# Attention pipeline, norms inside the projections, and one mixer stage in a two-block network on one Trainium2 core

## The chip, the core and the metric

The kernel runs on one core of one Trainium2 chip. A core has five engines that run beside each other and meet only at semaphores: TensorE (PE in the profile, PEld for its weight loads) multiplies matrices into PSUM, VectorE (DVE), ScalarE (ACT) and GpSimd (POOL) work on vectors, and SyncE (SP) issues nearly all transfers. The metric is the device time of one execution in microseconds (us). Everything is in 32-bit floating point.

## What is computed

Two blocks over 256 latent tokens of width 1024 follow each other; the first also carries 256 context tokens. Cut to what matters here (`rms` is a norm over the features with a gain):

```
first:  u = rms(h) * (1 + scale) + shift          # layer 0, 512 tokens
        h += gate * (delta_rule(u) gated) @ w_out
        u = rms(h) * (1 + scale) + shift          # layer 1
        q, k, v, z = split(u @ w_in);  q, k = rms per head;  rope on the latent ones
        h += gate * (softmax(q k / sqrt(128)) v * silu(z)) @ w_out      # 8 query, 2 key heads
        x = rms(h)                                # final norm of the first block
second: p = rms(x) @ w_in                         # SSD, RWKV, HGRN and 3 x 1024 gate columns
        y_b = branch_b(p_b) @ w_branch_b          # b = SSD (normed), RWKV, HGRN
        x += (sum_b sigmoid(p_gate_b) * y_b) @ w_out
        g, v = split(rms(x) @ ffn_w_in);  x += (silu(g) * v) @ ffn_w_down
        return rms(x)
```

## The kernel before

Features lie on the 128 partitions, tokens along the free axis, so a tensor of width 1024 is eight tiles `[128, tokens]`. `h` and `u` hold 512 columns (context, latent). All weights come as one stream of 512 KB chunks, in the order in which they are used, into a ring of two sets of six slots (`Stream`). Each chunk is eight 128x128 blocks, one output tile of a 1024-deep product. SyncE loads the next group while TensorE uses the present one; how far it is ahead is set by waits on a count of finished tiles.

The program is a row of stages (`stage`): in each, every engine has its own list of instructions in a fixed order, written out by hand, with semaphore waits between the lists; at a stage's end all engines meet. Nothing plans the order at run time. On VectorE and ScalarE each instruction in a `Chain` waits for the one before it.

Around the change:

- `linear` is a projection stage: TensorE accumulates output tiles in PSUM banks, VectorE takes each away with the given `evacuate`. `project`, `residual_linear` (adds to `h`) and `gated_linear` (multiplies a gate) are made of it.
- `feature_norm` is a stage of its own: eight squares on ScalarE, seven adds on VectorE, column sums by TensorE, mean on VectorE, power -1/2 on GpSimd (`inverse_root`, L148), `spread` by TensorE, eight or sixteen scalings on VectorE (L455), for the modulated norm also sixteen biases on ScalarE (L430). It runs six times behind the prelude: after the DeltaNet output, after the attention output (final norm of the first block), before the SSD projection, on the SSD output ahead of the RWKV inputs, ahead of the FFN, and at the end.
- Attention: all 16 query and z tiles and 4 key and value tiles are projected first; `attention_keys` is a stage; `attention_heads` is a loop of four stages, one for each pair of query heads, each from the query norm to the gated output.
- `rwkv_inputs` makes the RWKV operands out of 14 projected tiles, with small products on TensorE.
- `BesideGroups` and `Beside` put products of a later projection into TensorE's list between the steps of a stage; ScalarE copies the tiles out, or takes tanh(x/2) of them for a gate. The 24 gate tiles are made beside `hgrn_heads`. The SSD heads make 16 tiles for RWKV beside themselves, of which two are products with columns of zeros.
- The end of the second block's mixing: three `gated_linear` stages, one stage on VectorE that adds the three, `residual_linear`, the norm, `swiglu`, `residual_linear`, the norm, and `finish`, which stores `out` with one DMA.

Of the kernel before, what the change touches and what calls it, by code (L numbers as in the profile page):

```python
# [16 lines left out]
F32 = mybir.dt.float32  # L17
# [4 lines left out]
P = 128  # L22
D = 1024
# [176 lines left out]
class Stream:  # L200
# [89 lines left out]
    def in_stage(self, count, per_group, summed, block):  # L290


        first = self.set

        @block.sync
        def _(sp):
            for g in range(count):
                other = (first + g + 1) % 2
                if g:
                    sp.wait_ge(summed, g * per_group)  # L300
# [4 lines left out]
            sp.wait_ge(summed, count * per_group)  # L305
# [105 lines left out]
def feature_norm(nc, bank, C, h, u, g_cols, mod, streams, sq, rs, gs):  # L411


    lo, n = streams[0][0], sum(x[1] for x in streams)
    tiles = n // P
    with stage(nc, "squared added summed mean root spread scaled") as (s, block):
        @block.gpsimd
        def _(pool):
            inverse_root(nc, pool, C, rs[:, 0:tiles], s["mean"], s["root"])

        @block.scalar
        def _(act):
            for k in range(KT):
                nc.scalar.activation(sq[:, k, 0:n], h[:, k, lo:lo + n], ACT.Square).then_inc(s["squared"], 1)  # L424
            if mod is not None:
                link = Chain(act, s["act_own"])
                for k in range(KT):
                    for i, (t0, tn, m) in enumerate(streams):
                        act.wait_ge(s["scaled"], len(streams) * k + i + 1)
                        link(nc.scalar.activation(u[:, k, t0:t0 + tn], u[:, k, t0:t0 + tn], ACT.Identity, bias=mod[:, k, m:m + 1]))  # L430

        @block.tensor
        def _(pe):
            pe.wait_ge(s["added"], KT - 1)
            column_sums(nc, C, bank[0], sq[:, 0, :], tiles).then_inc(s["summed"], 1)
            pe.wait_ge(s["root"], 1)
            spread(nc, C, bank[1], rs, tiles).then_inc(s["spread"], 1)

        @block.vector
        def _(dve):  # L440
            link = Chain(dve, s["dve_own"])
            if mod is not None:
                for _, _, m in streams:
                    link(nc.vector.tensor_scalar(gs[:, :, m], mod[:, 8:16, m], 1.0, None, ALU.add))
                    link(nc.vector.tensor_tensor(gs[:, :, m], gs[:, :, m], g_cols, ALU.mult))
# [2582 lines left out]
```

## Time and profile before

| | |
|---|---|
| median of 3 runs | 2381.48 us (2377.84 to 2381.9) |
| the profiled execution | 2380.35 us |
| its span in the profile | 2378.6 us |
| TensorE busy, weight loads busy | 2021.5, 1484.7 us |
| VectorE, ScalarE, GpSimd busy | 1059.6, 577.9, 76.0 us |
| mean granted TensorE clock | 0.914 of full speed |
| moved by DMA | 183.72 MB |

The span runs from the first to the last record of the profiled execution. Busy time is time in which an engine has an instruction at work, not waiting. The granted clock is the share of TensorE's full 2.4 GHz; it has two levels, 1.0 and 0.5. A 32-bit product is two records in the profile. In a timeline, a line may merge several instructions of one kind (x8), and the brackets give the idle time ahead of it and what ended it.

### The profile page before, as it was taken

The numbers are of one execution on the slowest core, as the hardware profiler recorded it, in microseconds if no ns is written. First come the engines' busy times: TensorE is split into PE (matmuls) and PEld (weight loads), VectorE is DVE, ScalarE is ACT, GpSimd is POOL, SyncE is SP. The second block draws the span as 40 slices with busy tenths as digits, with TensorE's granted clock in tenths as the row PEclk, the third lists the DMA queues.
The fourth block names the chain that finished last, engine by engine and source line by source line (L and its number), as shares of the span: only waits on it lengthen the run. The fifth ranks groups of instructions, "written<-read, shape, count | busy, mean of one in ns | idle before, by whom it ended". The sixth has DMA issues, their size and how long they took to land. (4 is left out here: it accounts for less than half of the span.)

```text
span 2378.6 us, 40862 instructions
## 1 busy us (share of the span) xinstructions
PE 2021.5 (85%) x16732; PEld 1484.7 (62%) x16732; DVE 1059.6 (45%) x2136; ACT 577.9 (24%) x1248; POOL 76.0 (3%) x51
## 2 busy tenths in 40 slices
PE   5889898998989898896955687867989999879997
PEld 2356666565666656345633576644776798768886
DVE  4345756656575665102134318776445433211101
ACT  2033443434344343002012103222332321000000
POOL 0000110101010010000000000000000000000000
PEclk9889998999999998897967888986999999989998
DMA  8610101011010100212300132111012222324443
GB/s 332 266 54 2 55 1 56 1 55 55 2 55 1 55 1 2 106 71 76 107 0 0 71 118 107 71 66 41 29 55 94 82 101 85 110 106 156 162 159 124
DMA packets 50339, 183.72 MB, mean 77 GB/s; under 512 B 5744, under 2 KB 7152, under 8 KB 49648
## 3 DMA queue, kind: packets, MB, share of 16 engines
q1 hardware_dynamic: 50160, 181.18, 20.6%
q8 instruction: 132, 2.16, 0.4%
q14 instruction: 47, 0.39, 0.1%
HBM read 180.11 MB, written 1.05 MB: 76 GB/s over the span
## 5 line engine op out<-in xcount | busy, mean ns | idle before, releaser
L826 PE MATMUL banks<-u,w_ring 128*128 128x512 f32 x768 | 357.0, 602 | 6.6 <-PEq L195 6.6
L406 PE MATMUL banks<-u,w_ring 128*128 128x256 f32 x1088 | 248.4, 390 | 13.5 <-PEq L195 13.5
L406 PEld LDWEIGHTS banks<-u,w_ring 128*128 128x128 f32 x1088 | 212.4, 197 | 47.2 <-issue 17.8
L826 PEld LDWEIGHTS banks<-u,w_ring 128*128 128x128 f32 x768 | 141.7, 193 | 137.6 <-issue 134.5
L485 PE MATMUL banks<-u,w_ring 128*128 128x256 f32 (+1 forms) x640 | 158.7, 412 | 17.2 <-PEq L195 17.2
L485 PEld LDWEIGHTS banks<-u,w_ring 128*128 128x128 f32 x640 | 125.7, 197 | 49.9 <-issue 33.6
L485 PE MATMUL banks<-gated,w_ring 128*128 128x512 f32 (+1 forms) x384 | 141.0, 530 | 3.0 <-PEq L195 3.0
L485 PEld LDWEIGHTS banks<-gated,w_ring 128*128 128x128 f32 x384 | 74.0, 193 | 69.6 <-issue 66.3
L424 ACT ACTIVATE sq<-h 128x256 f32<-128x256 f32 (+1 forms) x40 | 14.5, 444 | 349.7 <-PEq L195 349.7
L853 DVE SCALAR_TENSOR_TENSOR acc<-raw,hc,acc 128x512 f32<-128x512 f32 x128 | 96.2, 752 | 4.6
L382 PE MATMUL banks<-u,w_ring 128*128 128x256 f32 x384 | 88.2, 380 | 0.0
L485 PE MATMUL banks<-ffn,w_ring 128*128 128x256 f32 x352 | 77.9, 385 | 3.0 <-PEq L195 3.0
L485 PEld LDWEIGHTS banks<-ffn,w_ring 128*128 128x128 f32 x352 | 68.1, 194 | 12.8 <-issue 3.4
L382 PEld LDWEIGHTS banks<-u,w_ring 128*128 128x128 f32 x384 | 70.6, 191 | 8.2
L1046 PE MATMUL banks<-const_base,a_t 128*128 128x128 f32 x128 | 28.8, 420 | 54.9 <-PEq L195 29.8
L1202 ACT ACTIVATE acc<-banks 128x512 f32<-128x512 f32 x80 | 47.8, 597 | 94.9 <-PE banks L1070 94.9
L2893 DVE SCALAR_TENSOR_TENSOR h<-banks,mod,h 128x256 f32<-128x256 f32 x24 | 10.9, 481 | 133.0 <-PE banks L485 133.0
L2855 DVE SCALAR_TENSOR_TENSOR ffn_tanh<-ffn_tanh,banks 128x256 f32<-128x256 f32 x22 | 9.2, 418 | 136.7 <-ACT ffn_tanh L2847 136.7
L1275 DVE TENSOR_TENSOR acc<-acc,banks 128x512 f32<-128x512 f32 x80 | 55.0, 688 | 26.7 <-PE banks L1086 24.8
L1271 DVE TENSOR_TENSOR y<-banks,const_base 128x512 f32<-128x512 f32 x80 | 55.3, 691 | 25.3 <-PE banks L1061 24.0
L1225 ACT ACTIVATE dec<-banks,hs 128x128 f32<-128x128 f32 x128 | 47.0, 367 | 70.7 <-PE banks L1143 67.6
L1086 PE MATMUL banks<-y,acc 64*64 64x64 f32 x2560 | 57.6, 225 | 7.6 <-ACT acc L1202 6.1
(468 smaller groups left out, 3248.8 us busy)
## 6 DMA issues: line engine op xcount, KB each, us to landing
w_ring<-in_w SPq DMA_DIRECT2D x323, 512.0 KB, 6.0
h<-in_h SPq DMA_DIRECT2D x2, 2048.0 KB, 9.5
const_base<-in_const SPq DMA_DIRECT2D x1, 1216.0 KB, 5.4
const_part<-in_const SPq DMA_DIRECT2D x1, 1024.0 KB, 4.9
out<-u SPq DMA_DIRECT2D x1, 1024.0 KB, 4.8
const_part<-in_const SPq DMA_DIRECT2D x1, 640.0 KB, 4.4
const_part<-in_const SPq DMA_DIRECT2D x1, 512.0 KB, 3.5
w_rows<-in_rows SPq DMA_DIRECT2D x1, 512.0 KB, 5.7
```

What stands on the lines that cost most here:

```text
L382: mm = self.nc.tensor.matmul(place, self.st.chunk(g % 2, slot)[:, P * k:P * k + P], self.src(k), start=(k == 0), stop=(k == KT - 1))
L406: last = nc.tensor.matmul(out, lhs[k], rhs[k], start=(k == 0), stop=(k == n - 1))
L424: nc.scalar.activation(sq[:, k, 0:n], h[:, k, lo:lo + n], ACT.Square).then_inc(s["squared"], 1)
L485: mm = nc.tensor.matmul(bank[q % banks][:, 0:n_tok], st.chunk(h, c)[:, P * b:P * b + P], src(k), start=(k == 0), stop=(k == k_tiles - 1))
L826: mm = nc.tensor.matmul(self.places[m % len(self.places)][:, :], st.slot(m)[:, P * k:P * k + P], u[:, k, :], start=(k == 0), stop=(k == KT ...
L853: link(nc.vector.scalar_tensor_tensor(out, raw[:, m, :, i:i + SEQ], hc[:, 5 * m + i:5 * m + i + 1], out, ALU.mult, ALU.add), self.s["conv" ...
L1046: mm = nc.tensor.transpose(tile(bank[2 * (c % 2) + c // 2], t), tile(a_t[:, c, :], t), C("ident"))
L1086: mm = nc.tensor.matmul(block_of(bank[2 * d + j], t, hb), invt_c[half(j), d, 2 * t + hb, :], prod[half(j), d, hb, t, :], start=True, stop= ...
L1202: link(nc.scalar.activation(invt_c[:, d].rearrange("p s e -> p (s e)"), bank[4 + d][:, :], ACT.Copy), s["t_out"])
L1225: link(nc.scalar.activation(tile(vn[:, d, :], j), tile(bank[2], 2 * d + j), ACT.Copy, scale=col(BETA, 2 * j + d, t)), s["vn_ready"] if j a ...
L1271: link(nc.vector.tensor_tensor(prod[:, d], both(sums(2 * d, 256)), mask(d, lv), ALU.mult), s["p_ready"])
L1275: link(nc.vector.tensor_tensor(by_chain(inv[:, d]), by_chain(inv[:, d]), both(sums(2 * d, 256)), ALU.subtract), s["t_ready"])
```

## The change

Five things are done together. The norms lose their stage: `residual_norm` is a projection whose squares and adds follow each tile, with root and scaling at its end (`NormTail`); for the end of the first block `DoubleTail` gathers the sums for both norms that follow each other in one pass. Attention is one stage: keys, four pairs in a software pipeline, and the eight z tiles in TensorE's list between its first steps; the key and value tiles are projected first. `rwkv_inputs` takes the norm of the SSD output and six gate tiles (two more come from the SSD heads in place of the zeros), so `hgrn_heads` makes 16 gate tiles. These first eight gates lie in `h`, whose content goes to a DRAM tensor `hold` meanwhile and comes back in the mixer. The three branches, their sum and the output projection are one stage (`mixer_out`). The output is stored in eight pieces behind the last scaling.

```diff
+class NormTail:
+    def square(self, act, link, k):
+        act.wait_ge(self.s["evacuated"], self.base + k + 1)
+        if k >= 3:
+            act.wait_ge(self.s["added"], k - 2)
+        out = self.sq[:, k % 2, 0:self.n] if k else self.acc[:, 0:self.n]
+        link(self.nc.scalar.activation(out, self.tile(k), ACT.Square), self.s["squared"])
...
+    def sums(self, pe):
+        pe.wait_ge(self.s["added"], KT - 1)
+        column_sums(self.nc, self.C, self.bank, self.acc, self.tiles).then_inc(self.s["sums"], 1)
+        pe.wait_ge(self.s["root"], 1)
+        spread(self.nc, self.C, self.bank, self.rs, self.tiles).then_inc(self.s["spread"], 1)
...
+class DoubleTail(NormTail):
...
+    def mean(self, dve, link):
...
+        dve.wait_ge(self.s["root"], 1)
+        link(self.nc.vector.tensor_tensor(self.rs2[:, :], first, first, ALU.mult))
...
+def residual_norm(nc, st, bank, C, count, per_body, src, k_tiles, h, lo, n, gate, work, finish, loaded=None, make=NormTail):
...
+            for m in range(KT):
+                dve.wait_ge(s["used"], m + 1)
+                gate(m, bank[m % banks], link, s["evacuated"])
+                if m:
+                    tail.add(dve, link, m - 1)
+            tail.add(dve, link, KT - 1)
+            tail.mean(dve, link)
+            more["vector"](dve, link)
...
 # modulated norm, after the DeltaNet output
+                            for k in range(KT):
+                                link(nc.vector.tensor_tensor(u[:, k, :], h[:, k, :], bank[7][:, :], ALU.mult), s["scaled"])
...
+                                    link(nc.scalar.activation(u[:, k, t0:t0 + tn], u[:, k, t0:t0 + tn], ACT.Identity,
+                                                              bias=nxt[:, k, c:c + 1], scale=gs[:, k, c:c + 1]))
...
 # attention, TensorE's list
+                extra.products(pe, 4)
+                pe.wait_ge(s["k_sq"], ATT_KV)
+                column_sums(nc, C, bank[7], ksq, ATT_KV * TT)
...
+                extra.products(pe, 12)
+                pe.wait_ge(s["root"], 1)
+                for h in range(ATT_KV + 1):
+                    spread(nc, C, bank[h], rc[:, TT * h:TT * h + TT], TT).then_inc(s["spread"], 1)
+                extra.products(pe, 6)
...
+                query_turn(0)
+                query_sums(1)
+                extra.products(pe, 18)
+                query_roots(1)
+                for n in range(4):
+                    scores(0, n)
+                extra.products(pe, 8)
+                query_turn(1)
+                extra.products(pe, 16)
+                for i in range(pairs):
                     for n in range(4):
+                        turn(i, n)
+                        if i + 1 < pairs:
+                            scores(i + 1, n)
+                        if i and n == 0:
+                            outs(i - 1, 1)
+                        if i + 2 < pairs and n == 0:
+                            query_sums(i + 2)
+                        if i + 2 < pairs and n == 1:
+                            query_roots(i + 2)
+                        if i + 2 < pairs and n == 3:
+                            query_turn(i + 2)
+                    outs(i, 0)
+                outs(pairs - 1, 1)
...
 # rwkv_inputs, TensorE's list
+            extra.products(pe, 2 * KT)
+            pe.wait_ge(*loaded)
...
+            pe.wait_ge(s["x_out"], 1)
+            extra.products(pe, KT)
...
+            pe.wait_ge(s["n_added"], KT - 1)
+            column_sums(nc, C, bank[6], sq[:, 0, :], ST).then_inc(s["n_summed"], 1)
+            extra.products(pe, KT)
+            pe.wait_ge(s["a_in"], 4)
+            extra.products(pe, KT)
             pe.wait_ge(s["root"], 1)
...
+            pe.wait_ge(s["n_root"], 1)
+            spread(nc, C, bank[6], roots, ST).then_inc(s["n_spread"], 1)
...
 # build
+        start_loads(nc, [(hold, early)], late)
...
-                hgrn_heads(nc, st, bank, banks, C2, cs, p_hg, lf, kf, cc("hgrn_norm_w"), yh, work, latent, gates, 24, 6)
+                hgrn_heads(nc, st, bank, banks, C2, cs, p_hg, lf, kf, cc("hgrn_norm_w"), yh, work, latent, gates[:, 8:24, :], 16, 4)
...
+def mixer_out(nc, st, bank, C, branches, early, gates, h, hold, reloaded, work, u, g_cols):
+    units = [(b, m) for b in range(4) for m in range(KT)]
+    through = [0, 4, 8, 16, 24, 28, 32]
...
+            for q, (b, m) in enumerate(units):
+                if q >= banks:
+                    pe.wait_ge(s["evacuated"], q + 1 - banks)
...
+                    if b == 3 and m == 0:
+                        pe.wait_ge(s["mixed"], k + 1)
...
+                if b == 3 and m == 0:
+                    dve.wait_ge(reloaded, 16)
+                dve.wait_ge(s["used"], q + 1)
+                if b < 3:
+                    link(nc.vector.scalar_tensor_tensor(own, own if b else early[:, m, :], 1.0, ps, ALU.add, ALU.mult), s["evacuated"])
+                    if b:
+                        link(nc.vector.tensor_tensor(mixed, mixed, own, ALU.add), s["mixed"] if b == 2 else None)
...
 # last norm and store
+                        for k in range(KT):
+                            sp.wait_ge(s["scaled"], k + 1)
+                            sp.dma_start(out[:, SEQ * k:SEQ * k + SEQ], u[:, k, CTX:TOK]).then_inc(late, 16)
```

## Rows read from the trace of the kernel before

**Rows 1.** the page, part 1: busy us, share of the span, instructions

```profile
PE 2021.5 (85%) x16732; PEld 1484.7 (62%) x16732; DVE 1059.6 (45%) x2136; ACT 577.9 (24%) x1248; POOL 76.0 (3%) x51
```

**Rows 2.** windows: busy us (instructions) by engine, granted clock, DMA share, GB/s

```profile
1205.00:1314.00 109.00, 65.95 (x216) 38.82 (x216) 47.07 (x108) 27.04 (x56) 4.03 (x4) 0.74 0.00 0
1600.00:1641.00 41.00, 21.82 (x84) 12.94 (x84) 30.42 (x52) 13.77 (x24) 4.46 (x2) 0.58 0.00 1
1880.00:2000.00 120.00, 120.00 (x782) 111.90 (x781) 48.34 (x147) 26.55 (x55) 2.27 (x3) 1.00 0.21 80
2015.00:2113.00 98.00, 88.27 (x384) 75.88 (x384) 18.89 (x34) 0.00 (x0) 0.00 (x0) 0.93 0.36 129
```

**Rows 3.** timeline, first output projection to the next: start, us, engine, work

```profile
1081.96 0.88 DVE L2893 SCALAR_TENSOR_TENSOR h<-banks,mod,h 128x256 f32<-128x256 f32 x2 [12.86 <-PE banks L485]
1083.39 4.26 ACT L424 ACTIVATE sq<-h 128x512 f32<-128x512 f32 x8 [123.37 <-PEq L195]
...
1089.75 1.87 PE L155 MATMUL banks<-const_base,sq 128*128 128x1 f32 x8 [7.83 <-DVE sq L448]
...
1094.25 8.23 DVE L455 SCALAR_TENSOR_TENSOR u<-h,gs,banks 128x256 f32<-128x256 f32 x16 [2.37 <-PE banks L162]
1094.77 8.65 ACT L430 ACTIVATE u<-u,mod 128x256 f32<-128x256 f32 x16 [7.11 <-DVE u L455]
1103.93 57.51 PE L485 MATMUL banks<-u,w_ring 128*128 128x256 f32 x256 [9.79 <-PEq L195]
...
1109.68 0.42 DVE L2879 COPY pqz<-banks 128x256 f32<-128x256 f32 x1 [7.20 <-PE banks L485]
1113.13 0.42 DVE L2879 COPY pqz<-banks 128x256 f32<-128x256 f32 x1 [3.03 <-PE banks L485]
```

**Rows 4.** timeline, last key/value tile to the attention's output projection

```profile
1190.23 0.69 DVE L2879 COPY pkv<-banks 128x512 f32<-128x512 f32 x1 [6.18 <-PE banks L485]
...
1191.86 1.06 PE L1358 MATMUL banks<-const_base,pkv 128*128 128x128 f32 x8 [1.67 <-PEq L2583]
...
1193.18 3.45 PE L155 MATMUL banks<-const_base,sq 128*128 128x1 f32 x16 [0.26 <-ACT sq L1349]
...
1314.92 27.89 PE L485 MATMUL banks<-gated,w_ring 128*128 128x256 f32 x128 [1.50 <-PEq L195]
```

**Rows 5.** timeline, attention output, two norms, SSD projection

```profile
1342.85 0.48 DVE L2893 SCALAR_TENSOR_TENSOR h<-banks,mod,h 128x256 f32<-128x256 f32 x1 [2.97 <-PE banks L485]
...
1344.64 3.19 DVE L448 TENSOR_TENSOR sq<-sq 128x256 f32<-128x256 f32 x7 [1.30 <-ACT sq L424]
...
1350.79 4.10 DVE L455 SCALAR_TENSOR_TENSOR h<-h,cols,banks 128x256 f32<-128x256 f32 x8 [1.63 <-PE banks L162]
...
1366.99 43.58 PE L485 MATMUL banks<-u,w_ring 128*128 128x256 f32 x192 [4.77 <-PEq L195]
```

**Rows 6.** timeline, SSD end to RWKV heads; last, GpSimd in RWKV output

```profile
1586.96 0.42 DVE L1765 TENSOR_TENSOR u<-ssd_th,ssd_z 128x256 f32 x1 [0.16 <-DVE ssd_th L1763]
...
1630.29 3.93 POOL L148 TENSOR_TENSOR rc_rw<-rc_rw,const_base 128x16 f32<-128x16 f32 x1 [36.18 <-DVE rc_rw L1875]
...
1640.43 0.52 POOL L1914 MEMSET rw_m_t<- 128x512 f32 x1 [6.20 <-POOLq L195]
...
1829.53 2.89 POOL L148 TENSOR_TENSOR st_rw<-st_rw,const_base 128x16 f32<-128x16 f32 x1 [188.58 <-DVE st_rw L2314]
```

**Rows 7.** timeline, mixer branches, output projection, FFN

```profile
2015.21 29.92 PE L485 MATMUL banks<-u,w_ring 128*128 128x256 f32 x128 [1.64 <-PEq L195]
...
2082.76 30.28 PE L485 MATMUL banks<-gates,w_ring 128*128 128x256 f32 x128 [7.47 <-PEq L195]
...
2125.32 54.95 PE L406 MATMUL banks<-u,w_ring 128*128 128x256 f32 x246 [4.78 <-PEq L195]
```

**Rows 8.** the DMA view: issues, KB each, median us to landing

```profile
out<-u SPq DMA_DIRECT2D x1, 1024.0 KB, 4.8
...
rope<-in_rope SPq DMA_DIRECT2D x1, 256.0 KB, 2.8
```

More of the change, by code:

```diff
@@ L288, in groups, with in_stage @@
             decorate(run)
-    def in_stage(self, count, per_group, summed, block):
+    def in_stage(self, count, per_group, summed, block, through=None, between={}):
         first = self.set
+        through = through or [per_group * g for g in range(count + 1)]
         @block.sync
@@ L299, in _ @@
                 if g:
[L300 removed]
+                    sp.wait_ge(summed, through[g])
                 if g == count - 1:
@@ L407, in accumulate @@
     return last
[L411 to L445, printed above, removed]
-            for k in range(1, KT):
-                dve.wait_ge(s["squared"], k + 1)
-                link(nc.vector.tensor_tensor(sq[:, 0, 0:n], sq[:, 0, 0:n], sq[:, k, 0:n], ALU.add), s["added"])
-            dve.wait_ge(s["summed"], 1)
-            link(nc.vector.tensor_scalar(rs[:, 0:tiles], bank[0][:, 0:tiles], 1.0 / D, EPS, ALU.mult, ALU.add), s["mean"])
-            dve.wait_ge(s["spread"], 1)
-            for k in range(KT):
-                for t0, tn, m in streams:
-                    scale = gs[:, k, m:m + 1] if mod is not None else g_cols[:, k:k + 1]
-                    link(nc.vector.scalar_tensor_tensor(u[:, k, t0:t0 + tn], h[:, k, t0:t0 + tn], scale,
-                                                        bank[1][:, t0 - lo:t0 - lo + tn], ALU.mult, ALU.mult), s["scaled"])
@@ L1478, in attention_heads @@
-        with nc.Fori(0, ATT_Q // 4) as pair:
-            for half in range(2):
-                body(pair * 2 + half, pair)
+        q_of = lambda i: flat(pqz[:, 2 * i:2 * i + 2, :])
+        z_of = lambda i: flat(pqz[:, ATT_Q + 2 * i:ATT_Q + 2 * i + 2, :])
+        tile = lambda a, t: a[:, P * t:P * t + P]
+        angle = lambda n: rope[:, SEQ * n:SEQ * n + SEQ]
+        over = lambda a: a.unsqueeze(1).to_broadcast([P, 2, SEQ])
+        roots_of = lambda i: rq[:, i % 2, :] if i else rc[:, ATT_KV * TT:]
@@ L1819, in _ @@
                     mm.then_inc(s["spread"], 1)
+            pe.wait_ge(s["n_root"], 1)
+            spread(nc, C, bank[6], roots, ST).then_inc(s["n_spread"], 1)
+            pe.wait_ge(s["gd"], 1)
+            for t in range(ST):
+                pe.wait_ge(s["x_out"], 4 + t)
+                nc.tensor.matmul(bank[(7, 4)[t]][:, :], ps[:, 13, P * t:P * t + P], g_up[:, :], start=True,
+                                 stop=True).then_inc(s["g_raw"], 1)
+            extra.products(pe, KT)
             pe.wait_ge(s["rk_ready"], 1)
@@ L2705, in build @@
         C, _ = tiles_of((), None)
[L2707 to L2713 removed]
+        hold = nc.dram_tensor("hold", (P, KT, SEQ), F32).ap()
+        early = h[:, :, CTX:TOK]
+        start_loads(nc, [(hold, early)], late)
         p_rw = p_hg = sb("p_next", [P, 16, SEQ])
```

627 lines of the change are left out of this document (422 added, 205 removed).

## The prediction

> **What bounds the kernel now.** I read the page's busy shares first: TensorE 85%, VectorE 45%, ScalarE 24% [rows 1]. That says only that TensorE is the engine to follow. The windows by stage come next, because the average hides two kinds of stage. In the HGRN stage TensorE is busy all the time at full clock (120.00 of 120 us, clock 1.00); in the attention bodies it is busy 65.95 of 109 us at clock 0.74, in the RWKV input stage 21.82 of 41 us at 0.58 [rows 2]. The reader should see that TensorE sets the end in the first kind, and a chain through all engines in the second. The chain view covers only the last norm and says nothing of the rest. So the timelines around each place that the diff touches come last, and give the terms. All matrix work is in order on TensorE, so time is saved wherever TensorE has nothing to do while a norm or a softmax runs.
>
> The unit of the sum: one 128x256 output tile of eight products takes 3.45 us (two evacuations at 1109.68 and 1113.13). The first after an idle stretch took 5.75 us (from 1103.93 to 1109.68) [rows 3], so leaving idle costs 2.3 us.
>
> **A. DeltaNet output and modulated norm.** Before, the last product ends at 1081.95 and TensorE's next projection starts at 1103.93, 22.0 us later [rows 3]. After, seven of eight squares and six of seven adds lie beside later tiles. Behind the last product remain: the gated add 0.88, one 512-wide square 0.6, one add 0.7 (seven of them fill most of the 6.4 from 1083.39 to 1089.75), handovers 0.2, which puts the column sums at 1084.4 where they stood at 1089.75. The path on to the scaling (mean, power, spread) is kept. The 16 ScalarE activations (8.65 us for 16) still come last, since eight 512-wide multiplies on VectorE take 5.8. First scaling op 0.7 where it was 0.5. Gain 5.3 - 0.2 = 5.1 us. Bounds 3 to 6.
>
> **B. Attention.** Before, from the last key/value evacuation's end (1190.92) to the output projection (1314.92) 124.0 us pass, and the eight z tiles, which are now done inside the attention, cost 8 x 3.45 = 27.6 in the projection ahead: 151.6 together [rows 3, 4]. After, one stage holds four head pairs in a software pipeline. TensorE's work in it at full rate: z 27.6; 16 scores x 0.86 = 13.8; 32 value products x 0.43 = 13.8; rotations 4.3; 24 column sums x 0.43 = 10.3 (sixteen records, eight sums, in 3.45); 24 spreads and 72 transposes x 0.14 = 13.4 (eight in 1.06); together 83. VectorE's per pair: 47.07 over four bodies, 11.8, less 1.3 for three copies that go, plus gaps, 11 us; ScalarE's 27.04 over four, 6.8, and 0.8 for z copies [rows 2]. A full pair takes TensorE 12.6. So TensorE is the bound if nothing blocks its order. Three things do. query_sums(1) waits for roped(0), which stands behind six key operations on VectorE: 3.5 us. query_turn waits for scaled(i+2), placed behind a maximum and a normalisation: about 1.2 twice. The last pair has no scores to lie beside: about 2, and the last gating 0.8. Small handovers make up 3. Stage change 0.9. Sum 83 + 3.5 + 2.4 + 2.8 + 3 = 94.7, so 57 us less. Lower bound of the gain: the four bodies stay chains of 27 us each (109 us for four [rows 2]) and only the z tiles hide, 27 us. Upper bound: no stall, 68. I take 57: each wait has about one slot (1.4 us or more) of slack, and the waits I found are counted.
>
> A row speaks of the power on GpSimd. Sixteen columns took 2.89 us while VectorE waited and 3.93 us beside VectorE operations on two SBUF tensors [rows 6]. The change moves nearly every power beside busy VectorE; the 12-column one in the head (about 2.3 alone) has 5.2 us of z products over it, the two in the pair loop (1.0 alone) 1.4 us. The Trainium skill, GPSIMD Engine Reference, section 8 "Key points", says that GpSimd shares its SBUF interfaces with VectorE and contends with instructions that read two SBUF inputs. By that rule, which the two rows bear out, the loop's powers would lose some 0.4 us each, under 1 us in all; without it nothing. Neither alters the sum.
>
> **C. Attention output, final norm of the first block, first norm of the second.** Before: last product 1342.8, next projection 1366.99, 24.2 us [rows 5]. After: add 0.6; two squares and two adds, the second of each behind the first, 1.6; sums, mean, power, spread 3.0 (1347.83 to 1350.79) and 0.4 for the second sums; eight scalings x 0.51 = 4.1, with the second root found beside them; eight more 4.1; stage change 0.6. 14.4 less 0.7 of overlap between the two chains, 13.7: gain 10.5. Bounds 8 to 12. The mean of squares of the normed tensor comes from three tiny VectorE operations (0.6), hidden behind the first spread.
>
> **D. RWKV inputs.** Before, from the last SSD product on VectorE (1587.38) to the next stage (1640.43) 53.0 us: a norm of 11 us and a barrier, then the stage [rows 6]. VectorE's list in the new stage: the old 30.4 busy [rows 2] with small gaps, plus seven adds (3.19 for seven [rows 5]) and eight scalings (4.1): 38.5. TensorE's list: six gate tiles 20.7, plus the old products, 21.8 at clock 0.58 [rows 2] and so about 15 at full rate. It runs in order, so the last steps wait: the norm's sums wait for the seven adds (about 25 us in), then two tiles (6.9), the head spreads (2.5), the norm's spread reach 36 us, where VectorE, ready at 32.7, waits 3.5. Then scaling, two products, bonus: 43.7. With 0.6 to enter and leave on either side 44.8: gain 8. Bounds: -6 (TensorE's list at the clock of this stage now, 0.58) to 12 (VectorE alone). I take 8, since TensorE now has work from the first microsecond.
>
> **E. HGRN.** Sixteen instead of 24 gate tiles. TensorE is busy 120 of 120 us at clock 1.00 there [rows 2], so eight tiles are worth 27.6. VectorE is busy 48 of those 120 us and ScalarE 27, and both feed a level two levels ahead, so neither comes near TensorE's remaining 93. Bounds 20 to 28. The SSD heads lose nothing: the two gate tiles that they now make replace two tiles of zeros.
>
> **F. Mixer.** Before: 2015.21 to 2113.04, 97.8 us [rows 7]. After: 24 tile-equivalents x 3.45 = 82.9 plus 2.3 for the start = 85.2. What goes: TensorE's idle time (9.7 of the 98 us [rows 2], 7.47 of it at the mix [rows 7]) and a second slow start. The last mixed tile is ready 1.1 us after its product, and TensorE has seven products (3.0) to do first. Gain 12.6. Bounds 10 to 13. The reload of the early gates' place (1 MB) is issued some 41 us in and needed at 59; 1 MB of the same pieces landed in 4.8 us [rows 8]. The spill lies beside a projection with a weight stream like the mixer's, 0.36 of the DMA engines' time [rows 2].
>
> **G. Second norm of the block.** 12.3 us from 2113.04 to 2125.32 [rows 7]; as in A, adds and squares go beside: gain 3.4. Bounds 3 to 4.
>
> **H. Last norm and store.** 3.4 as in G. The store goes out as eight pieces, one behind each scaling; the last (128 KB) should land in about 2.5 where the whole took 4.8, by the 2.8 of the 256 KB of rope [rows 8]: 2.3 more. Total 5.7. Bounds 3 to 7. The Trainium skill, DMA: Bandwidth & Descriptors, section "Anatomy of one DMA", gives a fixed cost of about 2.0 us plus bytes over 436 GB/s. By that the piece would take an estimated 2.3 us, and the 1 MB store 4.4; the trace's 4.8 is near it, and the sum would be the same within 0.3.
>
> **Sum.** 5.1 + 57 + 10.5 + 8 + 27.6 + 12.6 + 3.4 + 5.7 = 129.9. The profiled execution took 2380.35 (span 2378.6 and 1.75 around it), 1.1 under the median of 2381.48. 2380.35 - 129.9 = 2250.5, as a median 2251.6. I say 2252.
>
> **Rivals.** (1) The attention pipeline stays a chain, each pair waiting for its own softmax. For it: every handover in the bodies is on the path today. Against: scores of pair i+1 are issued before pair i is used. Gain of B 27: 2282. 13%. (2) HGRN becomes bound by its level chain, or the new list in D by TensorE's order; for it: D's list is nearly as long as VectorE's. Against: both other engines have over half of E's time free. 15 to 20 us less: 2270. 12%. (3) More gain: denser TensorE work avoids slow starts. Five stage starts at 2.3 each would give 2241. For it: the gaps shrink from 12 to 9 us; against: 9.8 us of idle at 1103.93 were enough for a slow start. 12%. (4) Slower: the full clock isn't granted to the filled stages. One mechanism: in attention, D, E and F TensorE has about 83 + 36 + 120 + 83 = 320 us of full-rate work, packed with short waits. At 1.2 GHz throughout, it costs 320 more and the kernel takes 2570; it breaks even at 130 us of such work at half rate. For it: clock 0.74 and 0.58 in two of these places now. Against: 1.00 over the 120 us of HGRN, whose list is of the same kind. 2%. (5) The edit doesn't shorten anything because the fill waits for weights: DMA carries 129 GB/s in the mixer and the pace of tiles never shows a wait; 1%.
>
> **Chances.** Forecast 60%, (1) 13, (2) 12, (3) 12, (4) 2, (5) 1. The likeliest's own range is 2245 to 2262; the range given reaches down over most of (3) and up to (1): 2238 to 2284. A measurement of this kernel tells about 0.2% (4.8 us). Faster 0.96, same 0.01, slower 0.03.
>
> **What would show it.** TensorE's clock over the attention stage at 0.95 or more and the stage near 94 us; the HGRN stage 27 us shorter with TensorE still busy throughout; one unbroken run of products over 85 us in the mixer; 14 us between attention output and SSD projection. Wrong: a pair period above 16 us, TensorE idle in HGRN, a TensorE wait for weights in the mixer or for the reload on VectorE.

## The result and the profile after

The changed kernel takes 2256.03 us (median of 4 runs, 2254.94 to 2257.24) where the kernel before took 2381.38 beside it (4 runs, 2377.84 to 2381.9): a ratio of 0.9477, 95% interval 0.946 to 0.9493. The forecast was 2252, its likeliest case 2245 to 2262. The profiled execution took 2255.24 us with a span of 2253.5, so 125.1 us of span went.

The page first, part 1 and the clock line of part 2 (a digit a slice of 56.3 us), against [rows 1]:

```profile
PE 1979.7 (88%) x16700; PEld 1460.5 (65%) x16700; DVE 1049.9 (47%) x2118; ACT 587.4 (26%) x1255; POOL 76.1 (3%) x50
...
PEclk9899999999899999989899888998999999999999
```

TensorE is busy 42 us less with nearly as many instructions: the work is the same, more of it at full clock. Its idle time fell by 83 us. Then the windows by stage (columns as in [rows 2]): attention, RWKV inputs, HGRN, mixer:

```profile
1157.00:1252.00 95.00, 81.96 (x382) 62.05 (x383) 45.44 (x100) 32.59 (x68) 5.29 (x4) 0.96 0.12 45
...
1519.80:1568.00 48.20, 38.87 (x186) 31.46 (x186) 38.67 (x73) 19.27 (x39) 5.62 (x3) 0.85 0.32 119
...
1787.00:1913.00 126.00, 121.87 (x832) 114.59 (x832) 61.01 (x182) 32.36 (x62) 2.96 (x4) 0.99 0.18 68
1913.00:1998.00 85.00, 84.81 (x384) 74.03 (x384) 21.99 (x52) 2.92 (x7) 0.00 (x0) 0.98 0.45 161
```

Attention went from clock 0.74 to 0.96, TensorE's list there is 82 us (forecast 83; see B below for why they are so near), and the mixer is one run without a gap. VectorE's work is what it was.

The timeline gives the borders of the stages. Of A (before: [rows 3]) and of C (before: [rows 5]):

```profile
1078.65 1.00 DVE L2778 SCALAR_TENSOR_TENSOR h<-banks,mod,h 128x256 f32<-128x256 f32 x2 [12.01 <-PE banks L3146]
...
1081.22 1.05 PE L155 MATMUL banks<-const_base,tail_acc 128*128 128x1 f32 x8 [2.67 <-DVE tail_acc L3045]
...
1085.53 10.10 ACT L2797 ACTIVATE u<-u,mod,gs 128x256 f32<-128x256 f32 x16 [5.17 <-DVE u L2791]
1096.15 7.34 PE L441 MATMUL banks<-u,w_ring 128*128 128x512 f32 x11 [11.51 <-PEq L195]
...
1279.65 0.48 DVE L2820 SCALAR_TENSOR_TENSOR h<-banks,mod,h 128x256 f32<-128x256 f32 x1 [2.05 <-PE banks L3146]
...
1293.89 2.47 PE L441 MATMUL banks<-u,w_ring 128*128 128x256 f32 x5 [7.40 <-PEq L195]
```

TensorE's waits inside the attention stage (a bracket names who ended each), up to the output projection that [rows 4] has at 1314.92:

```profile
1157.24 1.07 PE L1381 MATMUL banks<-const_base,pkv 128*128 128x128 f32 x8 [1.84 <-PEq L2692]
1178.77 1.21 PE L155 MATMUL banks<-const_base,att_qsq 128*128 128x1 f32 x8 [3.56 <-DVE pqz L1491]
...
1214.16 1.12 PE L1347 MATMUL banks<-pqz,const_first 128*128 128x512 f32 x2 [1.25 <-DVE pqz L1485]
1217.96 1.12 PE L1357 MATMUL banks<-kf,pqz 128*128 128x512 f32 x2 [0.52 <-DVE pqz L1491]
1228.59 1.12 PE L1347 MATMUL banks<-pqz,const_first 128*128 128x512 f32 x2 [2.26 <-DVE pqz L1485]
1232.39 1.12 PE L1357 MATMUL banks<-kf,pqz 128*128 128x512 f32 x2 [0.52 <-DVE pqz L1491]
...
1251.68 8.66 PE L3146 MATMUL banks<-gated,w_ring 128*128 128x256 f32 x39 [1.39 <-PEq L195]
```

And the RWKV input stage, the one that disappointed (before: [rows 6]):

```profile
1515.27 0.43 DVE L1832 TENSOR_TENSOR u<-ssd_th,ssd_z 128x256 f32 x1 [0.16 <-DVE ssd_th L1830]
1516.68 0.34 SPq L2684 DMA_DIRECT2D const_part<-in_const  x1
...
1518.95 0.43 SPq L2684 DMA_DIRECT2D w_rows<-in_rows  x1
...
1519.83 0.17 DVE L1949 TENSOR_TENSOR rc_rw<-cols 128x14 f32<-128x14 f32 x1 [4.14 <-PEq L225]
...
1540.03 2.42 PE L1881 MATMUL banks<-const_part,tmp_rw 128*128 128x2 f32 x16 [3.50 <-DVE lw_rw L1963]
...
1545.33 0.98 PE L155 MATMUL banks<-const_base,tmp_rw 128*128 128x1 f32 x4 [2.88 <-DVE tmp_rw L1970]
...
1546.17 9.78 PE L386 MATMUL banks<-u,w_ring 128*128 128x256 f32 x32
...
1558.34 4.10 DVE L1986 SCALAR_TENSOR_TENSOR u<-u,cols,banks 128x256 f32<-128x256 f32 x8 [5.72 <-PE banks L162]
...
1565.91 0.52 POOL L2023 MEMSET rw_m_t<- 128x512 f32 x1 [15.26 <-POOLq L195]
```

In the kernel before, SyncE issued the same five loads while the norm's stage ran, and VectorE entered the input stage 0.96 us after its last scaling:

```profile
1588.22 0.34 SPq L2575 DMA_DIRECT2D const_part<-in_const  x1
...
1590.51 0.43 SPq L2575 DMA_DIRECT2D w_rows<-in_rows  x1
...
1600.02 0.17 DVE L1851 TENSOR_TENSOR rc_rw<-cols 128x14 f32<-128x14 f32 x1 [0.96 <-PEq L2583]
```

The account, each part between the same two events of both traces, in us:

| part | before | after | gain | forecast |
|---|---|---|---|---|
| A, DeltaNet output's last tile to projection | 22.0 | 17.5 | 4.5 | 5.1 |
| B, projections and attention | 211.0 | 155.5 | 55.5 | 57 |
| C, attention output and two norms | 52.1 | 42.2 | 9.9 | 10.5 |
| D, last SSD product to RWKV heads | 53.0 | 50.2 | 2.8 | 8 |
| E, HGRN | 154.8 | 125.8 | 29.0 | 27.6 |
| F and G, mixer and norm | 110.1 | 93.4 | 16.8 | 16.0 |
| H, down projection, norm, store | 96.5 | 89.0 | 7.5 | 5.7 |
| unchanged stages together | | | -0.8 | 0 |

The unchanged stages moved by 3.3 (all up to the first output projection), -1.4 (SSD), 0.3 and -1.7 (RWKV heads and output) and -1.2 (first half of the FFN).

### The profile page after: what moved, and what is told of

It reads as the page before. It is cut to its first block and busy times, and to the rows that moved or that the text cites. A ratio compares the mean times of both kernels' runs of the same rounds, so it can differ in the third digit from the quotient of the medians.

```text
span 2253.5 us, 40621 instructions
## 1 busy us (share of the span) xinstructions
PE 1979.7 (88%) x16700; PEld 1460.5 (65%) x16700; DVE 1049.9 (47%) x2118; ACT 587.4 (26%) x1255; POOL 76.1 (3%) x50
## 5 line engine op out<-in xcount | busy, mean ns | idle before, releaser
L410 PE MATMUL banks<-u,w_ring 128*128 128x256 f32 x1088 | 248.8, 391 | 14.8 <-PEq L195 14.8
L410 PEld LDWEIGHTS banks<-u,w_ring 128*128 128x128 f32 x1088 | 212.4, 197 | 48.7 <-issue 18.9
L780 PEld LDWEIGHTS banks<-u,w_ring 128*128 128x128 f32 x768 | 141.1, 192 | 136.6 <-issue 133.4
L386 PE MATMUL banks<-u,w_ring 128*128 128x256 f32 x480 | 118.8, 400 | 5.4 <-PEq L225 5.4
L441 PE MATMUL banks<-u,w_ring 128*128 128x256 f32 (+1 forms) x384 | 102.1, 430 | 20.2 <-PEq L195 20.2
L386 PEld LDWEIGHTS banks<-u,w_ring 128*128 128x128 f32 x480 | 94.0, 203 | 20.1 <-issue 7.6
L441 PEld LDWEIGHTS banks<-u,w_ring 128*128 128x128 f32 x384 | 75.4, 197 | 46.9 <-issue 38.0
L3146 PEld LDWEIGHTS banks<-ffn,w_ring 128*128 128x128 f32 x352 | 68.0, 193 | 12.9 <-issue 3.3
L1246 DVE SCALAR_TENSOR_TENSOR rn<-banks,hs,v_t 128x128 f32<-128x128 f32 x96 | 33.7, 351 | 65.4 <-PE banks L1087 62.8
L3040 ACT ACTIVATE tail_sq<-h 128x256 f32<-128x256 f32 (+1 forms) x28 | 13.2, 470 | 194.3 <-DVE h L2778 91.7
```

The source lines that it names most:

```text
L386: mm = self.nc.tensor.matmul(place, self.st.chunk(g % 2, slot)[:, P * k:P * k + P], self.src(k), start=(k == 0), stop=(k == KT - 1))
L410: last = nc.tensor.matmul(out, lhs[k], rhs[k], start=(k == 0), stop=(k == n - 1))
L441: mm = nc.tensor.matmul(bank[q % banks][:, 0:n_tok], st.chunk(h, c)[:, P * b:P * b + P], src(k), start=(k == 0), stop=(k == k_tiles - 1))
L780: mm = nc.tensor.matmul(self.places[m % len(self.places)][:, :], st.slot(m)[:, P * k:P * k + P], u[:, k, :], start=(k == 0), stop=(k == KT ...
L1246: link(nc.vector.scalar_tensor_tensor(tile(resid[:, d, :], j), tile(bank[0], 2 * d + j), col(NEG_EG, 2 * j + d, t), v_t[:, t, j, :], ALU.m ...
L3146: mm = nc.tensor.matmul(bank[m % banks][:, 0:n], st.chunk(g % 2, c)[:, P * (at % 8):P * (at % 8) + P], src(k), start=(k == 0), stop=(k == ...
```

## The experiments

All start from the changed kernel; medians in us, ratios against the kernel before, which ran beside each of them. The changed kernel did not run beside them, so whole times are compared by the ratio. None of the small edits made alone (nor the norm's own stage) is apart from the changed kernel's 0.946 to 0.9493 by its interval. What a small edit did is read in its own stage, since stages with the same code differ between kernels: the attention stage, from TensorE's first product to the output projection, takes 92.8 to 97.2 us in nine of them, with its clock between 0.93 and 0.98.

**Attention undone.** The functions and projections of the kernel before are put back:

```diff
-project(nc, st, bank, 1, 4, lambda k: u[:, k, :], TOK, pkv)
-project(nc, st, bank, 2, 4, lambda k: u[:, k, CTX:TOK], SEQ, pqz)
-attention(...)
+project(nc, st, bank, 4, 4, lambda k: u[:, k, CTX:TOK], SEQ, pqz)
+project(nc, st, bank, 1, 4, lambda k: u[:, k, :], TOK, pkv)
+attention_keys(...); attention_heads(...)
```

> The changed kernel with the attention of the kernel before (projections of queries and gates in 16 tiles ahead, keys in a stage, four bodies). Theory: the 55.5 us of this part come from softmax, norms and rotations lying beside TensorE's own list; so all of it goes back, 2311.5 us (2308 to 2315), the bodies at 27 us each with a granted clock near 0.74, and no other stage moves by more than 2 us. Rival 1: part of the gain belongs to the neighbours (the norm ahead, the dense projection behind it, a higher clock in what follows); then less comes back, near 2300, or the output projection and the SSD part change. Rival 2: a busy VectorE beside it costs other work in the new stage, so that the parts alone are worth more than 57: above 2316.

Measured 2312.88 (2309.68 to 2316.49), ratio 0.972 (0.9697 to 0.9743); from projection to output projection 1096.38 to 1307.41, 211.0 us again. The window over the bodies is the old one, clock 0.73:

```profile
1197.00:1307.00 110.00, 67.34 (x216) 40.13 (x216) 47.04 (x108) 27.04 (x56) 4.03 (x4) 0.73 0.00 0
```

The theory holds: the 55 us belong to this part and to none beside it. How they divide among the pipeline, the hidden z tiles and the single stage no run tells.

**No early gates.**

```diff
-hgrn_heads(..., latent, gates[:, 8:24, :], 16, 4)
+hgrn_heads(..., latent, gates, 24, 6)
-    extra.products(...)          # in rwkv_inputs, all six tiles
-start_loads(nc, [(hold, early)], late)
```

> The changed kernel without the early gates: the RWKV input stage makes no gate tiles (the norm stays in it), HGRN makes all 24, nothing is spilled or reloaded. Theory: HGRN goes back to 154.8 us (29.0 more). The RWKV input stage is held by TensorE's list with its six tiles and by the entry behind the loads; without both VectorE's list bounds it: from the last SSD product to the next stage 41 us in place of 50.2. Net 20 more, 2276 us. Rival 1: the input stage is bound by VectorE as it stands, the tiles are free there: it stays near 50 and the kernel takes 2285. Rival 2: HGRN was not bound by its tiles: below 2265.

Measured 2275.78 (2274.21 to 2283.55), ratio 0.9569 (0.9544 to 0.9594). HGRN takes 1779.76 to 1934.48, 154.7 us. The input stage takes 42.5 us (1516.68 to 1559.14): VectorE enters 0.74 us after the last SSD product, and waits 1.4 us for the norm's spread instead of 5.7:

```profile
1517.42 0.17 DVE L1928 TENSOR_TENSOR rc_rw<-cols 128x14 f32<-128x14 f32 x1 [0.74 <-DVE u L1832]
...
1551.55 4.10 DVE L1965 SCALAR_TENSOR_TENSOR u<-u,cols,banks 128x256 f32<-128x256 f32 x8 [1.36 <-PE banks L162]
```

So six tiles cost 7.7 us in D: 3.4 by the entry, since the barrier that stood behind the five loads goes with the tiles' weight loads, and 4.4 by the wait. Their move out of HGRN is worth 19.8 by the medians (21.2 by these two stages).

**Mixer in its old stages as well** (three `gated_linear`, the sum, the output projection; the norm still rides on the last).

> The kernel without early gates, and the branches, the mix and the output again as separate stages (the norm behind the output stays in its projection). Theory: against the kernel without early gates 13 us more (three stage changes with a slow start of TensorE, and the mix of 7.5 us with TensorE idle): 2289 us if that one takes 2276. Rival: most of the 13 us came from the weights being loaded further ahead in one stage and not from the idle time; then the stages are again 98 us but their idle time is no more than 5 us. Rival 2: under 8 us, if the reload of the early gates' place in the changed kernel was the cheaper arrangement for another reason.

Measured 2288.66 (2285.05 to 2296.6), ratio 0.9621 (0.9593 to 0.9649): 12.9 more than without early gates; from HGRN's end to the FFN 105.7 us against 93.7. TensorE's line shows where:

```profile
1934.66 29.45 PE L441 MATMUL banks<-u,w_ring 128*128 128x256 f32 x128 [1.64 <-PEq L195]
1965.14 14.05 PE L441 MATMUL banks<-yr,w_ring 128*128 128x256 f32 x64 [1.03 <-PEq L195]
1980.22 14.05 PE L441 MATMUL banks<-yh,w_ring 128*128 128x256 f32 x64 [1.02 <-PEq L195]
2001.74 30.04 PE L3142 MATMUL banks<-gates,w_ring 128*128 128x256 f32 x128 [7.47 <-PEq L195]
```

Two gaps of 1.0 and one of 7.5 make 9.5 of the 12.0 us; 2.2 more are the half clock behind the 7.5 (30.04 us for 128 records that take 27.86 at full clock). Since the kernel without early gates has the one-stage mixer without spill and reload and takes the 93.7 us that the changed one takes (93.4), spill and reload cost nothing that shows.

**SSD norm in its own stage** (`feature_norm` ahead of `rwkv_inputs`; the gate tiles stay).

> The changed kernel with the SSD norm again in a stage of its own ahead of the RWKV inputs; the six gate tiles stay in the input stage. Theory: the merged norm gained little, since it brought two waits of TensorE and VectorE (2.9 and 5.7 us), 7.3 us of VectorE's work and an entry that waits for the loads' issue: from the last SSD product to the next stage 53.6 us in place of 50.2, 2259.5 us. Rival 1: the merge saves the whole stage of 12.6 us less what VectorE gets: 8 us or more, 2264 or above. Rival 2: it saves nothing, 2256, or costs: below 2255.

Measured 2264.82 (2258.36 to 2267.29), ratio 0.951 (0.9485 to 0.9536). The stage pair takes 54.4 us (1520.41 to 1574.80), 4.2 more: near the theory. The whole is 8.8 more by the medians, though the intervals of the ratios still touch; 2.8 of the rest stand in the attention stage at clock 0.93 (97.2 us), unchanged code. So the merge is worth 4.2 by its stage; that the whole moved further is put down to the clock by that window only, and is otherwise open. Here the five loads again lie beside the norm's stage, and VectorE enters the input stage 0.58 us after the last scaling.

**Entry of D.**

```diff
+st.begin(6)                      # barrier and weight loads
 loads = start_loads(nc, [pair, (up[0:64 ...
-    st.begin(6)                  # in rwkv_inputs
```

> The changed kernel with one step moved: SyncE issues the six weight loads of the RWKV input stage, with the barrier before them, ahead of the five loads of constants. Theory: TensorE and VectorE enter 4.1 us after the last SSD product because the barrier stands behind the issue of five loads (some 3 us); with the barrier first they enter after about 0.9, and the constants, needed 9 us into the stage, are still in time. From the last SSD product to the next stage 47 us in place of 50.2; 2253 us. Rival 1: the constants now land behind 3 MB of weights, the low-rank products wait for them, and the gain is lost or turns into 2 us more (2256 to 2258). Rival 2: the entry is 4 us for another reason and nothing changes: 2256.

Measured 2254.23 (2252.53 to 2257.87), ratio 0.9474 (0.9459 to 0.9488). The stage takes 47.3 us (1515.87 to 1563.21):

```profile
1517.13 8.83 PE L386 MATMUL banks<-u,w_ring 128*128 128x256 f32 x32 [2.55 <-PEq L225]
1527.76 4.17 PE L1869 MATMUL banks<-up_rw,ps_rw 64*128 64x512 f32 x5 [1.79 <-DMA w_rows<-in_rows]
```

The entry shrank from 4.1 to 1.3 us. The whole is not apart from the changed kernel by the intervals. The second line is rival 1, small: the constants land 1.8 us late for TensorE, which VectorE, the slower there, doesn't feel.

**TensorE's order in D.**

```diff
-pe.wait_ge(s["x_out"], 1); extra.products(pe, KT)
+pe.wait_ge(s["x_out"], 2); extra.products(pe, 2 * KT)
 ...                              # key norm's sums, SSD norm's sums
-extra.products(pe, KT)
 pe.wait_ge(s["a_in"], 4); extra.products(pe, KT)
```

> The changed kernel with one gate tile of the RWKV input stage moved on TensorE: from behind the norm's column sums to ahead of the sums for the key norm, where TensorE waits 3.5 us. Theory: from 1546 us on TensorE's list has no gap and ends the stage, with 9.8 us for two tiles at half clock; one tile less there starts the norm's scaling some 3 us earlier and ends the stage 3.5 to 4 us earlier: 46.5 us in place of 50.2, 2252.3 us. Rival 1: VectorE's list is the bound (its wait of 5.7 us is only slack): the stage stays at 50, 2256. Rival 2: the evacuation of the moved tile delays ScalarE's own list and the sums come later: 2257 or more.

Measured 2256.14 (2253.04 to 2262.5), ratio 0.9479 (0.9461 to 0.9497). The stage takes 46.8 us (1520.06 to 1566.83) and VectorE's wait fell from 5.72 to 2.24; the attention stage stood at 97.0 in this profile, and the whole shows no change.

```profile
1550.53 6.30 PE L386 MATMUL banks<-u,w_ring 128*128 128x256 f32 x16
...
1559.21 4.10 DVE L1985 SCALAR_TENSOR_TENSOR u<-u,cols,banks 128x256 f32<-128x256 f32 x8 [2.24 <-PE banks L162]
```

One tile in 6.3 us where one takes 3.45 at full clock: the half clock is in this place with either order.

**Order of the pair loop.**

```diff
 # VectorE, per n
+if n == 2: scaled(i + 2)
 negmax(i + 1, n)
+if n == 3: roped(i + 2)
 probs(...)
-if n == 2: scaled(i + 2)
-if n == 3: roped(i + 2)
 # TensorE: query_turn(i + 2) at n == 2 in place of 3
```

> The changed kernel with the order of the pair loop altered: VectorE normalises the queries of pair i+2 before the third maximum and adds the rotation before the fourth pair of probabilities, and TensorE rotates behind the third scores. Theory: the waits of TensorE for VectorE (1.25, 2.26 and twice 0.52 us in the profile of the changed kernel) come from this order, not from VectorE's load: at least 3 us of them go, 2253 us. Rival 1: VectorE (11 us busy of a pair's 14.4) is so near to the bound that the waits turn up at the maxima and transposes: no more than 1 us gained. Rival 2: the rotation in the way of the fourth maximum makes the exponentials late: 2258 or more.

Measured 2258.55 (2253.16 to 2263.82), ratio 0.948 (0.9462 to 0.9499): nothing in the whole. From the loop's first transpose to the output projection 46.1 us against 46.6; of the four waits 0.33, 1.93 and 0.33 us are left. The kernel with all edits (below), whose loop did not meet a half-clock stretch, has the same waits and takes 44.3, so the order gives 2.3 us, less than forecast. In this kernel's own trace a half-clock stretch inside the loop took most of that away (the rotation at 1235.57 took 1.97 us for 1.12).

**Scale and bias.**

```diff
-tensor_tensor(u[:, k, :], h[:, k, :], bank[7][:, :], ALU.mult)                    # VectorE, 8 of 512
+scalar_tensor_tensor(u, h, gs[:, k, c:c + 1], bank[7], ALU.mult, ALU.mult)       # 16 of 256
-activation(u, u, ACT.Identity, bias=nxt[:, k, c:c + 1], scale=gs[:, k, c:c + 1])
+activation(u, u, ACT.Identity, bias=nxt[:, k, c:c + 1])
```

> The changed kernel with the modulated norm's scale taken back to VectorE: sixteen products with a column scale there, and sixteen additions of a column on ScalarE. Theory: a ScalarE activation of 128x256 with a scale column and a bias column takes 0.63 us, one with a bias column alone 0.54 as in the kernel before; ScalarE's chain of sixteen ends this norm, so it is 1.4 us shorter, and the first one starts 0.15 earlier: from the last product to the projection 16 us in place of 17.5, 2254.5 us. Rival: the activations are as long with the bias alone in this place, since they share tiles with VectorE; then VectorE's sixteen of 0.51 pace them and nothing is gained: 2256.

Measured 2255.51 (2247.18 to 2258.11), ratio 0.9462 (0.9442 to 0.9482). From the first scaling to the projection 9.7 us (1090.99 to 1100.69) against 11.4:

```profile
1090.99 8.23 DVE L2792 SCALAR_TENSOR_TENSOR u<-h,gs,banks 128x256 f32<-128x256 f32 x16 [2.36 <-PE banks L162]
1091.56 8.61 ACT L2799 ACTIVATE u<-u,mod 128x256 f32<-128x256 f32 x16 [5.92 <-DVE u L2792]
```

16 activations in 8.61 against 10.10: the scale column costs 93 ns each. The Trainium skill, ScalarE: Activation LUTs, section "What ACT_TABLE_LOAD costs", gives about 93 ns for each pointer operand of one column; the trace agrees. The whole part A is 16.8 us, since the column sums fell to half clock here (1.86 us for 1.05).

**One store.**

```diff
-for k in range(KT): sp.wait_ge(s["scaled"], k + 1); sp.dma_start(out[:, SEQ * k:SEQ * k + SEQ], u[:, k, CTX:TOK])
+sp.wait_ge(s["scaled"], KT); sp.dma_start(out[:, :], u[:, :, CTX:TOK])
```

> The changed kernel with its output stored in one piece behind the last scaling, as in the kernel before, in place of eight. Theory: the last 128 KB piece landed 1.9 us after its issue, the 1 MB store of the kernel before took 4.8; so the end of the kernel (last product to the end of the span, 11.1 us) becomes 14.0 us, 2259 us. Rival: the 7.5 us gained there come from the leaner norm and one stage less, the pieces give 1 us or less: 2257.

Measured 2260.86 (2256.97 to 2264.29), ratio 0.9483 (0.9464 to 0.9501). From the last residual addition to the end 13.9 us (2245.95 to 2259.8) against 11.0 (2242.53 to 2253.5): the pieces give 2.9. The ratio of the whole is 0.9483 to the changed kernel's 0.9477, so this rests on the stage.

**Four edits together** (entry, order in D, pair loop, scale).

> The changed kernel with four edits tried one by one: weight loads and barrier ahead of the constants, one gate tile moved ahead of the key norm's sums, the norm's scale taken back to VectorE, the new order in the pair loop. Theory: the stages' gains add, since each lies on the path: 3.0 + 3.5 + 1.7 + 0.6 = 8.8 us, 2247 us. Rival 1: in the input stage entry and order overlap (the constants land only 10.6 us after the entry and set the pace of what follows), so 3 us less: 2250. Rival 2: the gains are eaten by the clock, which has moved unchanged stages by 1 to 3 us between kernels: 2253.

Measured 2249.47 (2246.03 to 2258.6), ratio 0.9441 (0.9419 to 0.9462). D takes 43.7 us (1517.74 to 1561.45), 6.5 less as in the theory, the pair loop 44.3, 2.3 less, part A 16.8. By its median 6.6 us under the changed kernel, by the intervals not yet apart from it.

**TensorE kept busy in the norms.**

```diff
+self.fill(self.fills[0])         # products of constants, result unread
 pe.wait_ge(self.s["added"], KT - 1)
 column_sums(...)
+self.fill(self.fills[1])
 pe.wait_ge(self.s["root"], 1)
 spread(...)
+self.fill(self.fills[2])         # 4+2+16, 2+2+10, 2+2+7
```

> The changed kernel with products of constants, whose result nobody reads, on TensorE in the idle places of the norms: ahead of and behind the column sums and behind the spread (22, 14 and 11 products of 256 columns in the three norms that are followed by a projection). Theory: after about 9 us or more with little to do TensorE is granted half clock and gets the full one back only some us into the next stage; kept busy it starts at full clock, which saves 2.4 us behind the first norm, 1 to 1.5 behind each of the others, and 0.8 where the column sums ran at half: 5 us, 2251 us. Rival 1: the granted clock falls there all the same or falls elsewhere instead: 2256. Rival 2: the fill itself runs at half clock and delays the sums, the spread and the next stage: 2259 or more.

Measured 2256.43 (2250.0 to 2259.95), ratio 0.9459 (0.944 to 0.9479): no gain in the whole that is clear of the intervals. The windows tell the three places apart. Behind the third norm TensorE starts at full clock, and the FFN's first half takes 155.2 us for 158.0. Behind the second it starts at half as before. Behind the first it starts at full clock, which falls to half within about 1 us and stays there until 1105 (the first two lines):

```profile
1100.60:1101.10 0.50, 0.50 (x2) 0.26 (x3) 0.00 (x0) 0.00 (x0) 0.00 (x0) 1.00 0.00 0
1102.00:1104.00 2.00, 2.00 (x4) 0.69 (x3) 0.00 (x0) 0.00 (x0) 0.00 (x0) 0.50 0.94 354
...
1296.90:1301.00 4.10, 4.09 (x10) 3.29 (x11) 0.00 (x0) 0.00 (x0) 0.00 (x0) 0.50 0.68 211
...
2010.50:2014.00 3.50, 3.46 (x16) 3.11 (x17) 0.00 (x0) 0.00 (x0) 0.00 (x0) 1.00 0.69 204
```

What TensorE did before differs: it had been idle 3.41 and 3.19 us in the first two places, 1.77 in the third. The number of products differs too, and the first fill itself began at half clock (1088 to 1091), so these rows don't single out the idle time.

**The four edits with longer fills** (4+2+19, 2+2+14, 2+2+7).

> The kernel with the four edits, and the idle places of the three norms filled with products of constants: 25, 18 and 11 products, so that TensorE's last gap ahead of the next stage is under 2 us each time (where it was 3.4 and 3.2 us, behind the first two norms, the next stage still began at half clock; where it was 1.8 us it began at full clock). Theory: it is the idle time right ahead that costs the clock; all three stages begin at full clock: 2.9 us behind the norm ahead of the feed-forward part, 1 to 2.4 behind each of the others, 2244 us. Rival 1: the two places fall to half clock whatever is filled in: only the 2.9 us are gained, 2246.6. Rival 2: the longer fill is itself partly at half clock and ends behind the norm, which puts the next stage back: 2249 or more.

Measured 2241.13 (2237.06 to 2244.63), ratio 0.9405 (0.9392 to 0.9418): 14.9 us under the changed kernel, and the intervals are apart. TensorE's idle times ahead of the three projections are 1.60, 0.42 and 1.78 us, and all three start at full clock:

```profile
1099.00:1105.00 6.00, 4.40 (x12) 2.01 (x11) 0.40 (x1) 1.29 (x3) 0.00 (x0) 1.00 0.50 174
...
1295.00:1301.00 6.00, 6.00 (x30) 5.28 (x29) 0.42 (x1) 0.00 (x0) 0.00 (x0) 1.00 0.85 259
...
1998.38 3.91 PE L410 MATMUL banks<-u,w_ring 128*128 128x256 f32 x17 [1.78 <-PEq L195]
```

The same code behind them takes 29.0 (31.9 in the kernel with four edits), 43.4 (45.7) and 155.1 (158.0) us: 8.0 us. The middle 2.3 of them are not kept. The second fill ran at half clock for most of its length (first line below) and so ended 1 us too late, which costs 0.9 (43.3 us from output projection to SSD projection for 42.4). And the small products behind the SSD projection met a clock of 0.52 where they had met 0.91, and took 6.65 us for 4.01 (the last two lines, this kernel and the one with four edits). From the attention's output projection to the last SSD product the two kernels take 263.5 and 263.6 us. The first and the third place give 5.7 of the 6.4 us between the two spans.

```profile
1285.40:1290.40 5.00, 5.00 (x13) 3.98 (x13) 4.64 (x11) 0.00 (x0) 0.00 (x0) 0.50 0.00 0
...
1338.02 6.65 PE L1589 MATMUL banks<-w_dt,u 128*128 128x32 f32 x32 [1.76 <-PEq L2690]
...
1342.23 4.01 PE L1589 MATMUL banks<-w_dt,u 128*128 128x32 f32 x32 [1.76 <-PEq L2690]
```

That the three projections start at full clock is confirmed. That the idle time right ahead is what costs the clock is not shown: the fills were also longer, and in the second place the clock fell all the same, inside the norm, and came back during the fill. That is the text's rival 2, in one place of three.

## Why the prediction was right, and where it was not

The reading was right: TensorE's order sets the end, and time is won where it had nothing to do. The parts gave 126.0 of the 129.9 us, in the places named, and the unchanged stages took 0.8 back. That 2256 lies so near to 2252 is in part luck: A to D fell 7.9 us short together (D alone 5.2), and E to H gave 4.0 more than forecast. The attention, the gate tiles, the mixer, the SSD norm and the store were each undone by a run; the norms of A, C and G were not, and their gains stand on the traces alone. What the text asked for is there: clock 0.96 over the attention, TensorE busy in HGRN but for 3.9 us (as many as before), 85 us of products in the mixer (1913.15 to 1998.0), 14.2 us between attention output and SSD projection. Rivals 1 and 5 are out by the windows; rival 4 too, the filled stages are at 0.85 to 0.99. Of rival 2 the first half is out (HGRN); its second half, D bound by TensorE's order, is what happened, at 3.4 us (the order undone) and not at 15 to 20. Rival 3 did not come by itself: every stage behind a norm still began at half clock, after 8 to 17 us with little to do. Its mechanism is real, as the first and third fill of the last experiment show, but has to be made.

**A.** Adds and squares went beside the tiles as said. Two sizes were off and cancel in part: the sixteen activations with scale and bias took 10.10 us, counted as the 8.65 of [rows 3]; the column sums ran at full clock, 1.05 for 1.87.

**B.** The sum was 94.7 us and 95.8 were measured by the same events. It names a stage change of 0.9 and leaves it out of the addition; 1.4 were measured. The column sums were counted at 0.43 each from a row at half clock [rows 4] and cost 0.23. The waits in the pair loop were counted as 1.2 twice and are 4.6 us: the rotation holds up the next scores too, and the second wait is 2.26. A pair takes 14.4 us, not 12.6 and a wait. The z tiles were counted at full clock, but ran through two half-clock stretches (24 records in 7.02 us and 36 in 9.51, where 16 take 3.45): 3.6 us more, which the column sums, 4.8 us less, hid. So the 82 us for 83 are in part luck. All told, 1.5 us too much gain.

**C.** 14.2 us for 13.7; nothing to mend.

**D.** This step failed: 8 forecast, 2.8 came. "With 0.6 to enter" is the wrong term: the stage is entered through a barrier that stands behind SyncE's issue of five loads, 4.1 us. In the kernel before, that issue lay beside the norm's stage [rows 6], which the change removed: a cover was gone, and it wasn't priced. Moving the barrier gave 2.9 us back. The second fault is TensorE's list: two tiles ahead of the spreads were put at 6.9 us and took 9.8, at half clock after waits of 3.5 and 2.9 us. So VectorE, ready 32.8 us in where 32.7 was forecast, waited 5.7, not 3.5. With entry and order changed (the four edits) the stage takes 43.7; the forecast was 44.8. The list was right, the way into it and the clock in it were not.

**E.** 29.0 for 27.6; undone, all of it comes back. TensorE's idle time in the stage is 3.9 us in both kernels, so the other 1.4 us are products that ran faster: the mean clock is 0.97 before and 0.99 after.

**F, G.** 16.8 for 16.0. The reload landed in 9.2 us, not 4.8, and still held up nothing.

**H.** 7.5 for 5.7. The pieces gave 2.9 for 2.3: the last landed in 1.9 us where 2.5 was taken. By the rule of the Trainium skill, DMA: Bandwidth & Descriptors, section "Anatomy of one DMA", it would be an estimated 2.3. The section fits that rule to transfers issued by GpSimd, while SyncE issues these; the trace is under it. Forgotten was the stage change between norm and store, 1.2 us before (last scaling's end 2372.0, issue 2373.24).

The powers on GpSimd of four columns took 1.01 us each, as before, but they didn't test the contention that the prediction weighed: while they ran VectorE was idle or reduced a tile out of PSUM. Where VectorE worked on two SBUF tensors, in D, it showed again: sixteen columns took 3.93 us, and two columns 1.17 where they take 0.70 alone.

## What to carry to other kernels

When work is laid into a stage, price the way in again: what SyncE issues ahead of the barrier was covered by the stage that goes away. In a list that is in order on TensorE, put the filling products into the waits, not behind them, and count at half clock what follows a wait of some us (3.5 and 3.56 us here, in D and in the attention). Where a norm leaves TensorE idle, products of constants that end shortly before the next stage can pay for themselves: they did in two places of three. Measure each place up to the end of the stage behind it, since a half-clock stretch can move there: the two fills that ended 3 us early gained next to nothing, and one that ran at half clock itself gave its whole gain back.

## Of the hardware, not expected

- With the same code a stage differed by up to 4.4 us between kernels (attention 92.8 to 97.2), by where the half-clock stretches fell. The Trainium skill, TensorE: Matmul & The Clock Gate, section "What's actually happening", says that the number of slow products at a start varies between runs of one kernel; the rows fit that, but they are of different kernels with one profile each.
- Behind fills of products TensorE began at full clock after idle times of 0.42, 1.60, 1.77 and 1.78 us, and at half after 3.19; after 3.41 it began at full and fell to half within about 1 us.
- The store of 128 KB in pieces landed in 1.9 us, one of 1 MB in 4.8; the reload of 1 MB beside a weight stream (DMA share 0.45) took 9.2.
